# A two-block transformer kernel: weights split one slab earlier, convolution blocks moved by DMA, queries split in two parts

## The reference

```python
h = _rmsnorm(x, g_mix[i]) * (1.0 + sc1[:, None, :]) + sh1[:, None, :]
proj = jnp.einsum('bsd,de->bse', h, w_in[i])
q, k, v, qi, ki, wi, cu = jnp.split(proj, split_at, axis=-1)
...
attn_out = _dsa_attention(q, k, v, qi, ki, wi)
conv_out = _conformer_conv(cu, conv_w[i], conv_b[i],
                           conv_norm_g[i], conv_norm_b[i])
mixed = jnp.concatenate([attn_out, conv_out], axis=-1)
x = x + gt1[:, None, :] * jnp.einsum('bse,ed->bsd', mixed, w_out[i])
```

## Time and profile before

| | |
|---|---|
| median of 3 runs | 2812.22 us (2811.51 to 2820.6) |
| profiled execution | 2813.73 us, of which the span of the trace is 2812.1 us |
| PE busy | 2643.6 us (94%) |
| DVE busy | 1339.8 us (48%) |
| ACT busy | 867.2 us (31%) |
| granted TensorE clock, mean | 0.973 of full |

### The profile page before, as it was taken

One profiled execution on the slowest core, in us unless ns is written; L12 is line 12 of the kernel. 1 busy time (PEld: TensorE's weight loads), 2 busy tenths in 40 slices (PEclk: granted clock), 3 DMA queues, 4 the chain that ended last, 5 costly groups with the idle time before them and its releaser, 6 DMA issues.

```text
span 2812.1 us, 28666 instructions
## 1 busy us (share of the span) xinstructions
PE 2643.6 (94%) x11363; PEld 2090.2 (74%) x11363; DVE 1339.8 (48%) x1629; ACT 867.2 (31%) x1133; POOL 234.7 (8%) x252
## 2 busy tenths in 40 slices
PE   5999999999999999999999977899999999999996
PEld 3887667877888888888765755565778888888884
DVE  5242666366334343346647877774453222232233
ACT  4111435333112021122325676555332121120221
POOL 0000222002112121120000000110000000000000
PEclk9999989999999999999899988999999999999997
DMA  3211010223222222231310100000201111111111
GB/s 119 79 45 56 34 60 26 74 81 137 77 84 95 72 89 78 83 105 54 126 34 15 38 31 15 1 1 15 97 30 53 47 51 46 52 45 52 45 53 67
DMA packets 45255, 166.23 MB, mean 59 GB/s; under 512 B 5751, under 2 KB 6007, under 8 KB 45111
## 3 DMA queue, kind: packets, MB, share of 16 engines
q1 hardware_dynamic: 27936, 101.07, 11.0%
q0 software_dynamic: 17216, 63.72, 6.6%
HBM read 151.80 MB, written 12.68 MB: 58 GB/s over the span
## 4 chain that ended last, share of the span: by engine, by line
PE 83%; DVE 8%; ACT 5%; issue 3%; DMA 0%; DVEq 0%; POOL 0%; ACTq 0%; POOLq 0%
PE G L1158 63%; PE G L1176 4%; PE TP L1581 2%; PE G L1352 2%; PE TP L1372 1%; PE G L1499 1%; PE TP L1325 1%; ACT TK L1004 1%; PE G L1515 1%; PE TP L1196 1%; DVE XP L2123 1%; PE TP L1469 1%; ACT T L990 1%; PE TP L1549 1%; PE TP L1377 1%
## 5 line engine op out<-in xcount | busy, mean ns | idle before, releaser
L1158 PE MATMUL G<-XH,whi 128*128 128x512 f32 x1712 | 539.7, 397 | 26.1 <-DVE wlo L1648 24.3
L1158 PE MATMUL G<-XL,whi 128*128 128x512 f32 x1712 | 530.4, 391 | 0.0
L1158 PE MATMUL G<-XH,wlo 128*128 128x512 f32 x1712 | 529.8, 391 | 0.0
L702 ACT ACTIVATE whi<-raw 128x1024 fp32r<-128x1024 f32 x184 | 193.7, 1053 | 732.1 <-PE G L1158 671.1
L1158 PEld LDWEIGHTS G<-XH,whi 128*128 128x128 f32 x1712 | 320.1, 189 | 98.2 <-DVE wlo L1648 28.7
L1158 PEld LDWEIGHTS G<-XL,whi 128*128 128x128 f32 x1712 | 323.2, 189 | 68.4
L1158 PEld LDWEIGHTS G<-XH,wlo 128*128 128x128 f32 x1712 | 323.0, 189 | 68.1
L1158 PE MATMUL G<-UH,whi 128*128 128x512 f32 x1024 | 316.8, 391 | 0.0
L1158 PE MATMUL G<-UL,whi 128*128 128x512 f32 x1024 | 315.4, 389 | 0.0
L1158 PE MATMUL G<-UH,wlo 128*128 128x512 f32 x1024 | 315.3, 389 | 0.0
L1648 DVE TENSOR_TENSOR wlo<-raw,whi 128x1024 fp32r<-128x1024 f32 x184 | 224.3, 1219 | 150.9 <-ACT whi L702 150.5
(11 more groups left out here) (304 smaller groups left out, 3192.7 us busy)
## 6 DMA issues: line engine op xcount, KB each, us to landing
raw<-slabs SPq DMA_DIRECT2D x184, 512.0 KB, 3.5
ADA<-ada POOLq DMA_DIRECT2D x48, 512.0 KB, 3.8
x_spill<-XT POOLq DMA_DIRECT2D x2, 4096.0 KB, 12.9
BIAS<-tab_spill POOLq DMA_DIRECT2D x8, 960.0 KB, 4.9
XT<-xT SPq DMA_DIRECT2D x8, 512.0 KB, 9.5
XRE<-xT POOLq DMA_DIRECT2D x8, 512.0 KB, 4.1
XRE<-x_spill POOLq DMA_DIRECT2D x8, 512.0 KB, 3.8
XT<-x_spill POOLq DMA_DIRECT2D x1, 4096.0 KB, 14.0
```

Source lines behind the costliest of these rows:

```text
L702: act.activation(whi[b][:, :, :].rearrange("p k n -> p (k n)"), raw[b][:, :], ACT.Copy).then_inc(hi_ready, 1)
L1158: last = pe.matmul(G[b][:, half, :], w[b][:, k, :], x[:, k, half * HALF:(half + 1) * HALF], start=(at_k == 0 and n == 0), stop=(at_k == KT ...
```

## The change

1. ACT's `hi` and DVE's `lo` of a slab are done one slab sooner: in section m they treat slab m+2, `hi` right behind the eviction of slab m. `lo` of slab 6 stands ahead of the index scores. Two bits are done beside slab 4, the last two beside slab 16.
2. The tiles of the convolution on PE are kept in order of phase (`CUQ`): the eviction and the gate write them so, reading in steps of four elements. The 16 blocks of a tile are then moved by 16 DMAs in SP's list (`to_phases`). Results are evicted by one instruction a group into `XP`, and four DMAs a group move them to `YC` (`to_channels`). `YC` is in order of phase too; the taps on DVE read and write it in hops (`in_time`), as `XH` and `XL` read `HC`. Slabs 16 on of the second projection up to the third output slab are loaded by single entries of SP's list between these.
3. ACT's copies into `WT` become 16 DMAs in POOL's list.
4. `BAND` has five buffers; bands 0 to 3 and groups 0 to 3 are placed later: groups 0 and 1 behind slabs 17 and 18, 2 and 3 among the first `least` products.
5. `query_high`, `query_low` and `key_low(1)` are done for 256 tokens first; the other 768 follow behind the first readings of attention.

```diff
@@ -257,6 +257,9 @@
+    by_phase = lambda t: t.rearrange("p (n q) -> p q n", q=PHASES)
+    CUQ = CU[:, :, :].rearrange("p j (q n) -> p j q n", q=PHASES)
+    LEAD_N = PAD // PHASES
@@ -392,6 +396,12 @@
+    PHASES_OF_TILE, OUT_OF_TILE = 16 * PHASES * PHASES, 16 * PHASES * PHASES
+    def band_of(n):
+        return BAND[n % 3] if n < PHASES else BAND[3 + n % 2]
@@ -407,8 +417,8 @@
-    bits_beside = {m: 2 if m <= 10 else 3 for m in range(5, 18)}
-    bits_beside[17] = BITS - sum(v for m, v in bits_beside.items() if m < 17)
+    bits_beside = {m: 2 if m <= 10 else 3 for m in range(4, 17)}
+    bits_beside[16] = BITS - sum(v for m, v in bits_beside.items() if m < 16)
@@ -491,10 +502,58 @@
-        with sp.Fori(0, (STREAM - 2) // 2) as t:
-            for j in range(2):
-                sp.wait_ge(lo_ready, t * 2 + (1 + j))
-                load(t * 2 + (2 + j), j)
+        first_loop, last_loop = (IN2 + 16 - 2) // 2, (OUT2 + 3 - 1) // 2
+        def next_slab(g):
+            sp.wait_ge(lo_ready, g - 1)
+            load(g, g % 2)
+        def load_pairs(first, end):
+            with sp.Fori(first, end) as t:
+                for j in range(2):
+                    sp.wait_ge(lo_ready, t * 2 + (1 + j))
+                    load(t * 2 + (2 + j), j)
+        def to_phases(j):
+            sp.wait_ge(glu_ready, j + 1)
+            sp.wait_ge(pool_seq, 3)
+            sp.wait_ge(roped, 10)
+            if j > 1:
+                sp.wait_ge(conv_out, OUT_OF_TILE * (j - 1))
+            for q in range(PHASES):
+                for g in range(PHASES):
+                    sp.dma_start(XP[j % 2][CB * q:CB * (q + 1), g, :], CUQ[CB * g:CB * (g + 1), j, q, :]).then_inc(phases_ready, 16)
+        def to_channels(j, g):
+            sp.wait_ge(conv_evicted, PHASES * j + g + 1)
+            if j == 0:
+                sp.wait_ge(conv_used, PHASES)
+                sp.wait_ge(wt_moved, 1)
+            for at_p in range(PHASES):
+                p = PHASES - 1 - at_p
+                sp.dma_start(YC[CB * g:CB * (g + 1), j, p * S // PHASES:(p + 1) * S // PHASES],
+                             XP[j % 2][CB * at_p:CB * (at_p + 1), g, 0:S // PHASES]).then_inc(conv_out, 16)
+        load_pairs(0, first_loop)
+        next_slab(IN2 + 16)
+        to_phases(0)
+        next_slab(IN2 + 17)
+        next_slab(IN2 + 18)
+        to_phases(1)
+        next_slab(OUT2)
+        next_slab(OUT2 + 1)
+        for j in range(PE_TILES):
+            for g in range(PHASES):
+                to_channels(j, g)
+            if j + 2 < PE_TILES:
+                to_phases(j + 2)
+        next_slab(OUT2 + 2)
+        load_pairs(last_loop, (STREAM - 2) // 2)
@@ -654,6 +714,12 @@
+        pool.wait_ge(wt_zero, 1)
+        for q in range(PHASES):
+            for g in range(PHASES):
+                first = PHASES + 1 - q
+                w = vecs[CB * g:CB * (g + 1), VCOL["conv_w"]:VCOL["conv_w"] + 4 * CONV_K].rearrange("p (j k) -> p j k", j=4)
+                pool.dma_start(WT[0][CB * q:CB * (q + 1), :, g, first:first + CONV_K], w).then_inc(wt_ready, 16)
@@ -969,12 +1035,13 @@
-            elif 1 < m < N_IN2 - 1:
-                hi_next(g, g % 2, g // 2)
...
-            act.activation(dst, Gf[g % 2], func, scale=scale).then_inc(psum_free[g % 2], 1)
+            by_q = dst is not None and len(dst.shape) == 3
+            act.activation(dst, by_phase(Gf[g % 2]) if by_q else Gf[g % 2], func, scale=scale).then_inc(psum_free[g % 2], 1)
+            if 0 < m < N_IN2 - 2:
+                hi(g + 2, g % 2, g // 2 + 1)
@@ -1006,27 +1073,22 @@
-        def phase_weights():
...
-                    act.activation(WT[0][CB * q:CB * (q + 1), :, g, first:first + CONV_K], w, ACT.Copy).then_inc(wt_ready, 1)
...
-            if n == PHASES:
-                act.wait_ge(wt_moved, 1)
...
-            for at_p in range(PHASES):
-                rows = slice(CB * at_p, CB * (at_p + 1))
-                act.activation(YC[CB * g:CB * (g + 1), j, PHASES - 1 - at_p::PHASES], out[rows, :], ACT.Identity,
-                               bias=phase_b[rows, 4 * g + j:4 * g + j + 1]).then_inc(conv_out, 1)
+            act.activation(XP[j % 2][:, g, 0:S // PHASES], out, ACT.Identity,
+                           bias=phase_b[:, 4 * g + j:4 * g + j + 1]).then_inc(conv_evicted, 1)
+        EARLY = 2 * P
+        def query_high(r, cols):
+            own = halves(r)[0]
+            act.activation(M2[r][own, :, cols], QT2[own, :, cols], ACT.Copy).then_inc(stack_hi, 1)
+        count_signs(bits_beside[4])
@@ -1036,13 +1098,8 @@
-                    step(m, dst=CU[:, j, PAD:PAD + S])
+                    step(m, dst=CUQ[:, j, :, LEAD_N:] if j < PE_TILES else CU[:, j, PAD:PAD + S])
...
-            if m >= 17:
-                conv_result(m - 17)
-            if m == 11:
-                act.wait_ge(eye_ready, 5 * PHASES)
-                phase_weights()
@@ -1052,15 +1109,16 @@
-        for r in range(2):
-            own = halves(r)[0]
-            act.activation(M2[r][own, :, :], QT2[own, :, :], ACT.Copy).then_inc(stack_hi, 1)
+        query_high(0, slice(0, EARLY))
+        query_high(1, slice(0, EARLY))
...
-        conv_result(2)
-        conv_result(3)
+        act.wait_ge(eye_ready, 5 * PHASES)
+        conv_result(0)
+        conv_result(1)
+        query_high(0, slice(EARLY, S))
@@ -1091,6 +1149,9 @@
+        query_high(1, slice(EARLY, S))
+        conv_result(2)
+        conv_result(3)
@@ -1126,7 +1187,7 @@
-            act.activation(XH[:, 4 + j, :], HC[j % 2][:, :], ACT.Copy).then_inc(x_hi, 1)
+            act.activation(XH[:, 4 + j, :].rearrange("p (n q) -> p n q", q=PHASES), in_time(HC[j % 2][:, :]), ACT.Copy).then_inc(x_hi, 1)
@@ -1520,11 +1581,11 @@
-            if m >= 15:
-                if m == 15:
+            if m >= 17:
+                if m == 17:
...
-                    conv_product(m - 15, block)
+                    conv_product(m - 17, block)
@@ -1538,8 +1599,8 @@
-            if p in (0, 4):
-                pe.wait_ge(stack_lo, 3 * r + 3)
+            if p in (0, 4, 16):
+                pe.wait_ge(stack_lo, (3, 6, 10)[min(p // 4, 2)])
@@ -1595,7 +1656,13 @@
-            for p in range(4 * MIN_AHEAD):
+            for block in range(BLOCKS):
+                conv_product(2, block)
+            for p in range(4):
+                least(p)
+            for block in range(BLOCKS):
+                conv_product(3, block)
+            for p in range(4, 4 * MIN_AHEAD):
@@ -2008,6 +2075,7 @@
+        lo(IN2 + 6, (IN2 + 6) % 2)
@@ -2098,52 +2166,43 @@
-        def key_low(r):
+        def key_low(r, cols=slice(0, S)):
...
-                dve.tensor_tensor(KL2[r][at_p, :], KT2[own, :], KS2[r][own, :].bitcast(F32), ALU.subtract).then_inc(stack_lo, 1)
-        def query_low(r):
+                dve.tensor_tensor(KL2[r][at_p, cols], KT2[own, cols], KS2[r][own, cols].bitcast(F32), ALU.subtract).then_inc(stack_lo, 1)
+        EARLY = 2 * P
+        def query_low(r, cols):
...
-            dve.wait_ge(stack_hi, 4 + r + 1)
-            dve.tensor_tensor(M2[r][other, :, :], QT2[own, :, :], M2[r][own, :, :].bitcast(F32), ALU.subtract).then_inc(stack_lo, 1)
-        def phases(j):
...
-            for q in range(PHASES):
-                for g in range(PHASES):
-                    dve.tensor_copy(XP[j % 2][CB * q:CB * (q + 1), g, :],
-                                    CU[CB * g:CB * (g + 1), j, q::PHASES]).then_inc(phases_ready, 1)
+            dve.wait_ge(stack_hi, 4 + r + (1 if cols.start == 0 else 3))
+            dve.tensor_tensor(M2[r][other, :, cols], QT2[own, :, cols], M2[r][own, :, cols].bitcast(F32), ALU.subtract).then_inc(stack_lo, 1)
...
-                dve.wait_ge(wt_ready, PHASES * PHASES)
+                dve.wait_ge(wt_ready, 16 * PHASES * PHASES)
+                dve.wait_ge(eye_ready, 5 * PHASES)
...
-            if n % PHASES >= 2 or n >= PHASES + 2:
-                dve.wait_ge(conv_used, n - 1)
-            dve.tensor_tensor(BAND[2 * (j > 0) + n % 2][:, :, :], eye[:, :].unsqueeze(1).broadcast_to([P, PHASES * BLOCKS, CB]),
+            if n == 3 or n >= PHASES + 2:
+                dve.wait_ge(conv_used, n - 2 if n == 3 else n - 1)
+            dve.tensor_tensor(band_of(n)[:, :, :], eye[:, :].unsqueeze(1).broadcast_to([P, PHASES * BLOCKS, CB]),
...
+        for _ in range(bits_beside[4]):
+            select_bit(bits.pop(0))
...
-            if m < N_IN2 - 1:
-                lo(IN2 + m + 1, (IN2 + m + 1) % 2)
-            if 16 <= m < 18:
-                band(m - 14)
+            if m < N_IN2 - 2:
+                lo(IN2 + m + 2, (IN2 + m + 2) % 2)
@@ -2157,27 +2216,22 @@
-                dve.tensor_tensor(CU[:, j, PAD:PAD + S], CU[:, j, PAD:PAD + S], SIG[:, :], ALU.mult).then_inc(glu_ready, 1)
+                dve.tensor_tensor(CUQ[:, j, :, LEAD_N:], CUQ[:, j, :, LEAD_N:], by_phase(SIG[:, :]), ALU.mult).then_inc(glu_ready, 1)
...
-            if m == 13:
-                phases(0)
-            if m == 14:
-                band(0)
-                band(1)
```

(36 more changed lines are left out.)

## The result

The median of 4 runs is 2792.66 us (2787.34 to 2795.42); the kernel before, on the same chip, had 2816.14 (2811.51 to 2820.6). The ratio is 0.9904, 95% interval 0.988 to 0.9928: faster, by about 1%. The prediction said 2790 (2780 to 2802). The profiled execution took 2793.15 us with a span of 2791.4, where the sum had 2791.3 for the execution. The medians differ by 23.5 us, the forecast by 22.4.

A forecast was written before the change was run, and what follows sets the result against it. DVE's list sets the pace from slab 12 to the end of the input projection, and PE waits. The profiled 2813.7 - 21.3 - 5.3 + 4.2 gives 2791.3 us, stated as a median of 2790, range 2780 to 2802.

The forecast's parts named there:

- a single gap of 9.6 us: After the input projection: PE idles once, 9.6 us, before the block of `least` products.
- Part 3: Start of attention, queries in two parts: step 1 at 1728.9 us instead of 1750.24, gain so far 21.3 us.
- Part 1: Second layer's input projection: weights one slab sooner, bits from section 4; slab 15 at 1645.2 us instead of 1662.6.
- Part 2: Blocks moved by SP's queue, 9.4 us a tile; hopping gates and taps 2.0 us; 0 to 2 us before the means.
- the prediction's last paragraph: Signs to check: wrong if taps pass 2.5 us, `whi` waits for a DMA, or the means wait for moved blocks.
- The split itself hides some 5 us: Start of attention: doing the queries in two parts hides some 5 us by itself.
- Part 4: Within attention: third tile's copies gain 4.3 us, shorter results about 4, dearer taps lose 3; net 5.3 gained.
- Part 5: Tail: hopping `XH` and `XL` start the output product 1.7 us later; 4.2 us lost in all.
- B: Rival, 0.16: hopping is dearer, taps cost 3.1 us, DVE bounds attention; time about 2803 us.
- C: Rival, 0.11: hopping costs nothing where DVE and ACT have slack; 2783 us, or 2779 with the clock staying up.
- D: Rival, 0.02: the loader's queue is the new bound; losing all 22 us needs 2.7 us per DMA, 2813 and up beyond.
- E: Rival, 0.03: bits keep DVE at the pace, the earlier split only moves the wait; 2806 to 2816 us.

The follow-up runs named there:

- e4: Changed kernel with the blocks copied between partitions by DVE again instead of the loader's queue; ratio 0.9957 to the kernel before.
- e11: Changed kernel with the 16 convolution weight copies on ACT again instead of POOL's DMAs; ratio 0.9923 to the kernel before.
- e7: Changed kernel with ACT's copies of the keys' high half put behind section 13's eviction and split; ratio 0.988 to the kernel before.
- e5: Changed kernel with ACT's split (`whi` of slab m+2) ahead of the eviction in each section; ratio 0.9883 to the kernel before.
- e2: Changed kernel with queries and the second key head's low half made whole again, ahead of the `least` products; ratio 0.9899 to the kernel before.
- e3: Changed kernel with DVE's taps of the last tile in straight order, output wrong there, same work; ratio 0.9922 to the kernel before.
- e9: Changed kernel with each block-moving DMA cut in two halves, 32 for a tile, same bytes; ratio 0.9912 to the kernel before.
- e13: Changed kernel with `whi` before evictions, keys' copies later, straight gates, taps over straight runs, `HC` in time order; 2777.49 us, ratio 0.9842 to the kernel before.
- e8: Changed kernel with the last tile by phase and each tap as up to two instructions over straight runs; ratio 0.9892 to the kernel before.

## Why the prediction was right, point by point

**What bounds the kernel.** Right: DVE's list, with ACT's `whi` in it, sets the pace to the end of the projection. Edits on it came back whole in three runs (e4 10.3 us of 10.2, e11 5.2 of 5.3, e7 4.8 of 4.7). One reading was short: "a single gap of 9.6 us" behind the projection was the second of two, with 8.45 us of waiting for DVE's `M` just ahead of it. The schedule of Part 3 holds both all the same, since it goes by DVE's ends.

**Part 1.** With the 1.9 us of the start taken off, slabs 14, 15, 16 and 18 started at 1627.7, 1645.5, 1662.9 and 1690.7; the schedule had 1627.4, 1645.2, 1662.7 and 1691.1. The waits were 2.63, 6.56 and 3.95 us and none at slab 17, where 2.5, 5.8, 4.7 and 2.2 were forecast. DVE's period in sections 6 to 10 was 13.07 us (13.1). The six us of spare time that the two extra bits were to take in the first window don't show there: DVE is busy 0.4 us more. The heads of sections 15 and 16 are shorter in the schedule than its 2.6 us, without a word; the rows agree, as `wlo` waits for nothing behind a band. The end of the projection came at 1705.8 for 1704.0: slab 18 at 1691.1 and its 10.95 us leave 2.0 us for the last group of convolution, which took 4.05. It cost nothing, since DVE was later still. The sum hid one thing. I wrote that `whi` becomes 0.9 us dearer in a section and added that up inside the schedule, but never stood it against the gain of the early split. It is 10.0 us of 12.3 (e5).

**Part 2.** Right in each price but one. SP 0.63 us a DMA (0.59), 10.1 a tile (9.4), landing 1.8; the load of slab 17 with 9.6 us to spare (11); evictions 1.00 us with no penalty, gates 2.00 (2.0), taps 2.09 (2.0). A result took 0.47 (0.38). The means waited 1.57 us for moved blocks. That is inside the 0 to 2 of Part 2, but the prediction's last paragraph calls such a wait a sign that it is wrong, and the sum has nothing for it: by that sign this term was missed, and it was small. The wait is 1.57 to 1.59 us in all kernels but e4 (1.88), so it does not touch the comparisons. The weights' way to POOL, which I counted in without a figure, is worth 5.2 (e11). The Trainium skill (Vector Engine (DVE) Microarchitecture Reference, section on measured stream behaviour on trn2) has 1.73 ns per column for one hopping source, 1.71 for the target, 1.76 for both sources (which the prediction counts as one port), 1.98 for all three, and 1.054 for straight operands. A duration here has a start in it, so what hopping adds is the better comparison: the gate, with one hopping source, takes 1997 ns for 1220, 0.76 more per column where the page's rows differ by 0.68; the tap, with one source and the target hopping, 2085 for 1281, 0.79 more, between the page's 0.68 and 0.93. The trace nearly agrees; where they differ, the measurement decides.

**Part 3.** Step 1 was forecast 21.3 us earlier and came 22.5 earlier. What failed is the aside "The split itself hides some 5 us": it is 1.3 (e2). Step 0 does start 6.7 earlier, but 5.4 of it return behind it, where the same work of DVE stands before readings 9 and 10, as the prediction itself had scheduled. The 5 us had no working, and the schedule of whole queries was never made; the sum did not rest on it. No run puts groups 2 and 3 of the convolution back into the projection, so what their new place is worth is not shown.

**Part 4.** 4.8 us for 5.3: the third tile 3.9 for 4.3 (e4), the taps -3.6 for -3 (e3). What is left, 4.8 - 3.9 + 3.6 = 4.5, holds the shorter results (my 4), less the 1.57 us of the means' wait, and whatever the clock gave back; no run tried them by themselves.

**Part 5.** The output product's start lost 39.3 - 37.6 = 1.7 us, as forecast, and the whole tail 4.7 for 4.2.

**Sum.** Behind slab 5's product -22.6 for -22.4. In it 1.2 us more at step 1 stand against 0.5 less within attention and 0.5 more lost in the tail. That the execution came within 1.9 us of the sum is in part luck: the stretch ahead of that point, which the sum took as fixed, moves by 12.7 us between these profiles.

**Rivals.** B: the taps stayed at 2.09, far from 3.1. C: the taps cost 3.6 us and the tail 4.7, where C had nothing. D: tried in e9. E: the bits kept DVE at the pace, but the gain was real.

Left open: what lowers the clock between 300 and 400 us more in some executions than in others, and what else moves the start of slab 5 (12.7 us in all); and why the means gain only 3.4 of the 4.8 us in e7.

## What to carry to other kernels

Where two engines hand a chain of small steps to each other, put the instruction that the other engine waits for first in each round, ahead of evictions, table loads and copies that only have to be done by the end of it; here this order alone was worth 10 us, most of the 12.3 that splitting a slab sooner could give. A copy moved from the pacing engine to an idle DMA queue was won whole here; work put off behind the first step gave 1.3 us of 6.7, since what followed had no room for it. Work out an aside as carefully as a term of the sum, by the schedule of the version without the edit.

## What the runs showed of the hardware that was not expected

A PSUM operand read in steps of 16 bytes costs ACT nothing (1003 ns for 1024 columns), while steps of 1 KB in SBUF nearly double its time (1994 ns for 1057, and 2.15 to 2.23 us for 1.23 with scale and bias, e13). DVE takes as long with one source in steps of 16 bytes (1997) as in steps of 1 KB (1996). Its tap with hopping source and target takes 2085 ns, two instructions over straight runs 1494 to 1588 (e8). DVE copies 32 x 264 elements to other partitions in some 320 ns (5.09 us for 16) from straight runs and in 410 where the source hops. A DMA of 32 rows kept SP busy 0.63 us with 264 columns and 0.65 with 132 (20.82 us for 32), so the price is per DMA.
